# Rotary partners of the index heads fetched two tiles to a transfer, and a sixth scratch buffer

## The chip, the core and the metric

The kernel runs on one core of one Trainium2 chip. The metric is the device time of one execution in microseconds (us). The core's engines run side by side: PE (TensorE: matmuls, with PEld its weight loads), DVE (VectorE), ACT (ScalarE), POOL (GpSimd), and SP, which computes nothing here and only issues DMAs. Each engine and each issue queue works through its own list in order; semaphores tie the lists together. An instruction that waits holds up all that stands behind it on its engine.

## What is computed

Two transformer blocks run one after the other over 256 tokens of width 2048, in float32. The first has latent attention, a gated convolution and two output projections. The second, where the change lies, puts 16 meta tokens in front (T = 272 columns) and has a sparse attention, whose keys are chosen by a small indexer, and a gated recurrence. Cut to the indexer:

```python
h = rms_norm(x, norm_g); proj = h @ w_in
q_a, k_a, v_a, z_a, q_i, k_i, w_i, q_b, f_b, i_b, z_b, gates = jnp.split(proj, cuts, axis=-1)
qi = apply_partial_rope(q_i.reshape(B, T, 16, 64), *rope_i)      # 16 index heads of 64
ki = apply_partial_rope(rms_norm(k_i, idx_k_norm_g)[:, :, None, :], *rope_i)[:, :, 0, :]
score = jnp.einsum('bqhs,bqh->bqs', jax.nn.relu(jnp.einsum('bqhd,bsd->bqhs', qi, ki)), wi)
_, sel = lax.top_k(score, 64)                                    # then attention over sel
```

`apply_partial_rope` turns only the first 16 of a head's 64 elements: element j of the first 8 is combined with element j + 8, its partner, and the other way round. The other 48 pass through.

## The kernel before

Everything is held transposed, features on the 128 partitions and tokens along the row. A weight matrix comes in as units of up to 1024 columns by 128 partitions (512 KB): SP loads a unit into one of four `w_raw` buffers (`load`, L1259), ACT rounds it into `w_hi` (L1665), DVE forms the rest `w_lo` (L1973), and PE multiplies in three passes, hi by hi, hi by lo and lo by hi. A `load` waits for the `w_lo` of the unit four before it. A unit of this part is 24 matmuls of 256 or 272 columns.

The order of all engines' work is written by a planner, `plan_work`. `run` walks over the phases' units; when the last unit of a column group is done, `evac` puts the copies out of PSUM into the plan (for instance L2079 on DVE). After each unit `pump` is called once. It moves every active job one step on (a job is a Python generator, a step ends at a `yield`), then starts one job from the queue `pending`, if fewer than three are active. What a step adds is placed in the lists of all engines at that point. So a job's steps are one unit apart, and the queue is first come, first served.

The phases around the change are `qi` (one group of 8 tiles, 16 units), `ki` (2 units), `ka` (8), `va` (8), `qa2` (16), `fb` (16), `ib` (16). The 8 tiles of `qi` hold two index heads each; all are evacuated at the last `qi` unit. Then, for each tile, a job `rope_later("qi", k, ...)` is queued: a step that does nothing, then `rope_swap` (four DMAs on SP's queue, L1300, which copy the partner rows of the tile into a scratch buffer), an empty step, and `rope`. `rope` is one multiply by the sines on DVE (L2116, waits for the DMAs) and a multiply and an add on POOL (L2546, L2549). One tile's four DMAs are those of `SWAPS["qi"]`: for each half of 64 partitions one of 8 rows and one of 56 rows, 128 rows of 1024 bytes in all.

The job of the index key, `ki_job`, is queued at the `ki` evacuation. Its steps are: transpose, row sum, (empty), spread and normalise, (empty), `rope_key`. `rope_key` does the turn by two PE products (rotated, L1326 from `con`, and doubled), two DVE multiplies (L2124, L2126) and two DVE adds (L2130, L2131). At its end it queues the 16 jobs `index_head(h)`; each has a PE product that waits for the key (`done["ki", 0]`, the second add) and for its tile, an ACT relu, and, a step later, two DVE multiply-adds. The selection (DVE, 9 steps) follows the last index head, and queues the 8 attention heads `attention2`. Key heads (`ka_job`, 4) and query heads (`qa_job`, 8) are jobs too, queued at their evacuations. The recurrence is queued only after `qb`, a phase behind `ib`.

Scratch buffers come from `Ring(5)`: a step that needs one takes the next, and waits for the end of its last use. PSUM has five banks for products; a tile's first matmul waits until the tile that had the bank before is evacuated.

Of the kernel before, what the change touches and what calls it, by code (L numbers as in the profile page):

```python
# [9 lines left out]
F32R = mybir.dt.float32r  # L10
# [6 lines left out]
P = 128  # L17
D = 2048
KT = D // P
S = 256  # L20
NMETA = 16
T = S + NMETA
# [124 lines left out]
class Plan:  # L147
# [6 lines left out]
    def add(self, kind, *args, marks="", dma="", **of):  # L154
        s = Step(kind, args, of)
        for names, by in ((marks, 1), (dma, 16)):
            for name in names.split():
                self.count[name] = self.count.get(name, 0) + by
                s.raised.setdefault(name, []).append((self.sem(name), self.count[name]))
        self.steps.append(s)  # L160
        return s
# [105 lines left out]
def plan_work(sem):  # L267
    plan = Plan(sem)
    add, done = plan.add, plan.done
    ph = phases()  # L270
    units = plan.units = units_of(ph)
    banks, side, scratch, heads = Ring(5), Ring(3), Ring(5), Ring(3)
    stats, prob, prob_t, prob_m = Ring(6), Ring(2), Ring(2), Ring(2)
    issued, lows = {"load": 0, "split": 0}, deque()
    pending, active, deferred = deque(), [], deque()
# [132 lines left out]
    def rope_later(kind, k, ready, tables, rest=0):  # L408
        yield
        if kind == "kr":  # L410
            rope_key(kind, ready, tables)
        else:
            yield from rope(kind, k, ready, tables)
        for _ in range(rest):
            yield
# [18 lines left out]
    s = add("load_rows", dma="ld_pos " + "ld_rows " * 10 + "ld_meta", zero=zero)  # L434
    done["pos"], done["rows"], done["meta_in"] = s["ld_pos"], s["ld_rows"], s["ld_meta"]
    b = side.take()
    s = add("pre_cols", marks="pre_t pre_cols", bank=b, loaded=pre)
# [295 lines left out]
    s = add("meta_rest", marks="op_lo", head=done["meta_head"], high=done["meta_hi"])  # L733
# [49 lines left out]
    s = add("load_late", dma="ld_late ld_lvl")  # L783
# [20 lines left out]
    def evac_ki(g, m, pb, got):  # L804
        s = add("ki", marks="evac", pb=pb, got=got)
        pending.append(ki_job(s["evac"]))
        return s["evac"]

    def evac_qi(g, m, pb, got):
        k = m  # L810
        s = add("qi", k, marks="evac", pb=pb, got=got)
        pending.append(rope_later("qi", k, s["evac"], "late"))
        return s["evac"]

    def ka_job(k, t):
# [160 lines left out]

    pending.append(level_masks())
    run(ph["qi"], evac_qi)
    run(ph["ki"], evac_ki)
    run(ph["ka"], evac_ka)  # L980
# [79 lines left out]
ODD = 16  # L1060
H2_STEP, H2_AT, MG2_AT = 320, 32, 80
H2_LOW, H2_REST = 12, 33 * 64
# [8 lines left out]
class Memory:  # L1071


    def __init__(self, nc, ctx, a):
        def sb(name, shape, dt=F32):
            return ctx.enter_context(nc.sbuf_tensor(name, shape, dt))
# [5 lines left out]
        hb_all = sb("hb", [P, ODD + 2 * KT * S + ODD], F32R)  # L1082
        hb = hb_all[:, ODD:ODD + 2 * KT * S].rearrange("p (k n) -> p k n", k=2 * KT)
        self.hb_hi, self.hb_lo = hb[:, 0:KT, :], hb[:, KT:2 * KT, :]
        ob_all = sb("ob", [P, 2 * KT * (T + ODD)], F32R)
        ob = ob_all[:, H2_AT + NMETA:H2_AT + NMETA + 2 * KT * S].rearrange("p (k n) -> p k n", k=2 * KT)
        self.ob_hi, self.ob_lo = ob[:, 0:KT, :], ob[:, KT:2 * KT, :]
        mg2 = ob_all[:, MG2_AT:MG2_AT + 2 * KT * S].rearrange("p (k n) -> p k n", k=2 * KT)
# [8 lines left out]
        self.rope1 = sb("rope1", [P, 2, S])  # L1097
        self.fac = sb("factor", [P, 3, T])
        self.small = sb("small", [P, 256])
        self.scratch = [sb(f"scratch{i}", [P, T])[:, :] for i in range(5)]  # L1100
        self.heads = [sb(f"head_factor{i}", [P, T])[:, :] for i in range(3)]
        self.acc_a, self.acc_b = sb("acc_a", [P, S])[:, :], sb("acc_b", [P, S])[:, :]
        psum = [ctx.enter_context(nc.psum_tensor(f"bank{i}", [P, 512], F32))[:, :] for i in range(8)]
# [140 lines left out]
def sync_engine(nc, m, a, plan, S_):  # L1244

    sp, dma = Stream(nc.sync, None), nc.sync.dma_start
    rows = lambda ap: ap.rearrange("(k p) -> k p", p=P)

    def load_pre(s):
        sp.wait_ge(*s.of["zero"])  # L1250
        dma(m.rows_in[ROWS["pre"]:ROWS["pre"] + 16, :], rows(a["pre_norm_g"])).then_inc(S_("ld_pre"), 16)

    def load(s):
        i, = s.args
        u = plan.units[i]
        sp.wait_ge(*s.of["free"])
        src = m.weights[u.phase.weight].rearrange("(k p) n -> p k n", p=P)[:, u.k0:u.k0 + u.nk, u.c0:u.c0 + u.cols]
        dst = m.raw[:, i % N_RAW, 0:u.size].rearrange("p (k n) -> p k n", k=u.nk)
        dma(dst, src).then_inc(S_(f"raw{i % N_RAW}"), 16)  # L1259

    def load_con(s):
        dma(m.con[:, P:], a["const_f"][:, P:L0]).then_inc(S_("ld_con"), 16)

    def load_rows(s):
        dma(m.pos_i, a["positions"]).then_inc(S_("ld_pos"), 16)
        sp.wait_ge(*s.of["zero"])
        for name, src, n in (("post", rows(a["post_norm_g"]), 16), ("norm2", rows(a["norm_g_2"][0]), 16),
                             ("conv", a["conv_w"].rearrange("c (k p) -> (c k) p", p=P), 48),
                             ("qa", rows(a["q_a_norm_g"]), 4), ("kva", rows(a["kv_a_norm_g"]), 4),
                             ("lb", a["hgrn_lb_logits_2"].rearrange("l (k p) -> (l k) p", p=P), 16),  # L1270
                             ("qn", a["q_norm_g_2"], 1), ("kn", a["k_norm_g_2"], 1),
                             ("on", a["hgrn_out_norm_g_2"], 1), ("ikn", a["idx_k_norm_g_2"], 1)):
            dma(m.rows_in[ROWS[name]:ROWS[name] + n, 0:src.shape[1]], src).then_inc(S_("ld_rows"), 16)
        dma(m.x_meta[0:NMETA, :], a["meta_tokens_2"]).then_inc(S_("ld_meta"), 16)

    def load_x_again(s):
        sp.wait_ge(*plan.done["mg_z"])
        sp.wait_ge(*plan.done["x_kept"])
        dma(m.XR.rearrange("p k n -> p (k n)"), m.x_dram).then_inc(S_("ld_xagain"), 16)

    def x1_keep(s):
        sp.wait_ge(*plan.done["x1", KT - 1])
        dma(m.x1_dram, m.XR.rearrange("p k n -> p (k n)")).then_inc(S_("ld_x1kept"), 16)

    def load_late(s):
        sp.wait_ge(*plan.done["mg", KT - 1])
        dma(m.late, a["const_f"][:, L0:CONSTS["late"][1]]).then_inc(S_("ld_late"), 16)
        dma(m.lvl_in, a["const_lvl"]).then_inc(S_("ld_lvl"), 16)

    def load_x1_back(s):  # L1290
        sp.wait_ge(*plan.done["x1_kept"])
        sp.wait_ge(*plan.done["mg2_z"])
        dma(m.xT2.rearrange("p k n -> p (k n)"), m.x1_dram).then_inc(S_("ld_x1back"), 16)

    def rope_swap(s):
        x, use = m.rope_of(*s.args)[0], s.of["scratch"]
        sp.wait_ge(*use.after)
        sp.wait_ge(*s.of["ready"])
        for to, of, n in SWAPS[s.args[0]]:
            dma(m.scratch[use.slot][to:to + n, 0:x.shape[1]], x[of:of + n, :]).then_inc(S_(f"ld_rot{use.slot}"), 16)  # L1300

    def out2(s):
        g, blk = s.args
        sp.wait_ge(*s["evac"])
        w = slice(g * 512, (g + 1) * 512)
        dma(a["out"][0, blk * P:(blk + 1) * P, w], m.OT[:, blk, w]).then_inc(S_("ld_out"), 16)

    def end(s):
        sp.wait_ge(*s.of["stored"])

    does = dict(load_pre=load_pre, load=load, load_con=load_con, load_rows=load_rows, load_x_again=load_x_again,
                x1_keep=x1_keep, rope_swap=rope_swap, load_late=load_late, load_x1_back=load_x1_back, out2=out2, end=end)
    for s in plan.steps:
        if s.kind in does:
            does[s.kind](s)
# [1357 lines left out]
```

## Time and profile before

| | us |
|---|---|
| median of 3 runs | 1908.15 |
| lowest, highest | 1906.74, 1909.43 |
| the profiled execution's own time | 1908.92 |
| its span, first to last instruction | 1907.6 |
| PE busy | 1890.0 (99%) |
| DVE, ACT, POOL busy | 1174.7 (62%), 880.1 (46%), 323.6 (17%) |
| DMA | 347.31 MB, mean 182 GB/s |

A timeline row reads: start in us, length in us, engine, line of the kernel, operation, what it writes <- what it reads, count; in brackets, the time for which the engine was idle before it, and what ended that. `SPq` is SP's issue queue; its rows are the time that issuing takes, not the transfer. The rows of the DMA issue table show the weight loads as 512.0 KB each, landing 3.8 us after their issue.

### The profile page before, as it was taken

The numbers are of one execution on the slowest core, as the hardware profiler recorded it, in microseconds if no ns is written. First come the engines' busy times: TensorE is split into PE (matmuls) and PEld (weight loads), VectorE is DVE, ScalarE is ACT, GpSimd is POOL, SyncE is SP. The second block draws the span as 40 slices with busy tenths as digits, with TensorE's granted clock in tenths as the row PEclk, the third lists the DMA queues.
The fourth block names the chain that finished last, engine by engine and source line by source line (L and its number), as shares of the span: only waits on it lengthen the run. The fifth ranks groups of instructions, "written<-read, shape, count | busy, mean of one in ns | idle before, by whom it ended". The sixth has DMA issues, their size and how long they took to land.

```text
span 1907.6 us, 37116 instructions
## 1 busy us (share of the span) xinstructions
PE 1890.0 (99%) x15758; PEld 1857.5 (97%) x15758; DVE 1174.7 (62%) x1709; ACT 880.1 (46%) x1265; POOL 323.6 (17%) x317
## 2 busy tenths in 40 slices
PE   9999999999999999999999999999999999999999
PEld 8999999999999999999999999999999999999987
DVE  7765665656554556755654766676467776655744
ACT  6544454544444444544454543446443333444543
POOL 3220110202110003400221243040011132110300
PEclk9999999999999999999999999999999999999999
DMA  7566555566666666666565565563564444666664
GB/s 262 165 211 182 158 154 165 167 188 191 197 191 195 198 190 188 194 204 193 196 232 195 177 217 168 149 178 119 156 187 140 138 141 142 183 199 195 193 232 154
DMA packets 180752, 347.31 MB, mean 182 GB/s; under 512 B 11742, under 2 KB 24410, under 8 KB 180058
## 3 DMA queue, kind: packets, MB, share of 16 engines
q1 hardware_dynamic: 178938, 340.67, 58.8%
q10 hardware_dynamic: 1648, 4.26, 0.6%
q8 instruction: 124, 2.03, 0.4%
q14 instruction: 42, 0.34, 0.1%
HBM read 334.89 MB, written 6.29 MB: 179 GB/s over the span
## 4 chain that ended last, share of the span: by engine, by line
PE 92%; DVE 3%; SPq 1%; issue 1%; DMA 1%; ACT 1%; POOL 1%; POOLq 0%; ACTq 0%; DVEq 0%
PE bank L1326 91%; DVE w_lo L1973 1%; SPq L1300 1%; DMA scratch<-arena 1%; DMA w_raw<-in_w_in 1%; ACT w_hi L1665 1%; DVE hb L2215 0%; SPq L1259 0%; POOL stats L2533 0%; DVE arena L2079 0%; DVE scratch L2079 0%; ACT L1733 0%; POOL scratch L2583 0%; PE bank L1547 0%; ACT ob L1825 0%
## 5 line engine op out<-in xcount | busy, mean ns | idle before, releaser
L1973 DVE TENSOR_TENSOR w_lo<-w_raw,w_hi 128x1024 fp32r<-128x1024 f32 (+2 forms) x644 | 792.8, 1235 | 460.5 <-ACT w_hi L1665 458.6
L1665 ACT ACTIVATE w_hi<-w_raw 128x1024 fp32r<-128x1024 f32 (+2 forms) x644 | 662.8, 1032 | 854.5 <-PE bank L1326 839.7
L1326 PE MATMUL bank<-hb,w_hi 128*128 128x256 f32 x5284 | 954.5, 278 | 1.7 <-DVE hb L1997 1.6
L1326 PEld LDWEIGHTS bank<-hb,w_hi 128*128 128x128 f32 x5284 | 813.8, 188 | 3.7 <-DVE w_lo L1973 2.2
L1326 PE MATMUL bank<-ob,w_hi 128*128 128x256 f32 (+1 forms) x4060 | 767.7, 283 | 5.0 <-DVE ob L2269 1.7
L1326 PE MATMUL bank<-hb,w_lo 128*128 128x256 f32 x2448 | 677.5, 277 | 0.0
L1326 PEld LDWEIGHTS bank<-ob,w_hi 128*128 128x128 f32 x4060 | 633.2, 188 | 9.1 <-DVE w_lo L1973 2.3
L1326 PE MATMUL bank<-ob,w_lo 128*128 128x256 f32 (+1 forms) x2224 | 621.6, 279 | 0.0
L1326 PEld LDWEIGHTS bank<-hb,w_lo 128*128 128x128 f32 x2448 | 460.9, 188 | 0.0
L1326 PEld LDWEIGHTS bank<-ob,w_lo 128*128 128x128 f32 x2224 | 418.4, 188 | 0.0
L1326 PE MATMUL bank<-w_hi,ob 128*128 128x512 f32 (+1 forms) x384 | 104.4, 359 | 1.0 <-DVE arena L2079 1.0
L1326 PE MATMUL bank<-arena 128*128 128x64 f32 (+4 forms) x578 | 89.9, 296 | 1.0 <-POOL arena L2623 1.0
L2593 POOL TENSOR_TENSOR arena<-scratch,arena 128x256 f32<-128x256 f32 x32 | 38.4, 1229 | 258.7 <-DVE scratch L2079 258.7
L1326 PEld LDWEIGHTS bank<-w_hi,ob 128*128 128x128 f32 x384 | 66.9, 188 | 12.2 <-DVE arena L2079 1.4
L1326 PEld LDWEIGHTS bank<-arena 128*128 128x128 f32 x578 | 74.3, 191 | 3.0 <-issue 1.2
L2079 DVE TENSOR_TENSOR scratch<-bank,factor 128x256 f32<-128x256 f32 (+1 forms) x132 | 52.4, 421 | 30.7 <-PE bank L1326 30.6
L1326 PE MATMUL bank<-w_lo,ob 128*128 128x512 f32 (+1 forms) x192 | 68.4, 356 | 0.0
L2566 POOL TENSOR_TENSOR arena<-arena,factor 128x256 f32<-128x256 f32 x16 | 19.2, 1233 | 257.6 <-DVE arena L2079 257.6
L2583 POOL TENSOR_TENSOR scratch<-scratch,head_factor 128x256 f32<-128x256 f32 x16 | 12.5, 784 | 225.2 <-ACT head_factor L1783 225.2
L2079 DVE TENSOR_TENSOR arena<-bank,factor 128x256 f32<-128x256 f32 (+1 forms) x86 | 34.1, 418 | 18.2 <-PE bank L1326 18.2
L1326 PEld LDWEIGHTS bank<-w_lo,ob 128*128 128x128 f32 x192 | 36.1, 188 | 5.8
L2586 POOL TENSOR_TENSOR arena<-scratch,arena 128x256 f32<-128x256 f32 x32 | 39.6, 1237 | 2.5
(241 smaller groups left out, 1019.6 us busy)
## 6 DMA issues: line engine op xcount, KB each, us to landing
w_raw<-in_w_in SPq DMA_DIRECT2D x436, 512.0 KB, 3.8
w_raw<-in_w_out SPq DMA_DIRECT2D x64, 512.0 KB, 4.2
w_raw<-in_w_o_conv SPq DMA_DIRECT2D x32, 512.0 KB, 4.0
w_raw<-in_w_o_mla SPq DMA_DIRECT2D x32, 512.0 KB, 4.0
w_raw<-in_w_branch SPq DMA_DIRECT2D x32, 512.0 KB, 4.4
w_raw<-in_w_kv_b SPq DMA_DIRECT2D x16, 512.0 KB, 4.6
w_raw<-in_w_q_b SPq DMA_DIRECT2D x16, 384.0 KB, 3.5
arena<-x_kept SPq DMA_DIRECT2D x2, 2048.0 KB, 9.0
```

What stands on the lines that cost most here:

```text
L1300: dma(m.scratch[use.slot][to:to + n, 0:x.shape[1]], x[of:of + n, :]).then_inc(S_(f"ld_rot{use.slot}"), 16)
L1326: return nc.tensor.matmul(dst, lhsT, rhs, start=start, stop=stop, skip_group_check=True)
L1665: act(dst, src, ACT.Copy).then_inc(S_("w_hi"), 1)
L1973: tt(low, src, high.bitcast(F32), ALU.subtract).then_inc(S_("w_lo"), 1)
L2079: tt(dst, m.proj[s.of["pb"]][:, 0:dst.shape[1]], factor, ALU.mult).then_inc(S_("evac"), 1)
L2566: tt(m.u_t[:, t, :], m.u_t[:, t, :], m.R, ALU.mult).then_inc(S_("conv_b"), 1)
L2583: tt(z, z, ring[s.of["head"].slot][:, 0:S], ALU.mult).then_inc(S_("silu"), 1)
L2586: tt(y, z, y, ALU.mult).then_inc(S_("gated"), 1)
L2593: tt(y, m.scratch[s.of["scratch"].slot][:, 0:S], y, ALU.add).then_inc(S_("merged"), 1)
```

## The change

The scratch ring has six buffers instead of five, and all six lie in one tensor, so that two neighbours can be named in one access pattern. `ob` is cut from 9216 to 8992 columns, which it doesn't use. The eight `rope_later("qi", ...)` jobs are replaced by one job, `index_ropes`, queued after the last tile's evacuation. After an empty step it goes over the tiles in pairs: it takes two neighbouring scratch buffers (never the last with the first), adds `rope_pair`, an empty step, and then the two `rope` steps of the pair, followed at once by the next pair's `rope_pair`. `rope_pair` issues four DMAs for two tiles, each with twice the bytes in as many rows of partitions. DVE's and POOL's work on a tile is as it was.

```diff
-    banks, side, scratch, heads = Ring(5), Ring(3), Ring(5), Ring(3)
+    banks, side, scratch, heads = Ring(5), Ring(3), Ring(6), Ring(3)
...
+    index_tiles = []
+
+    def index_ropes():
+
+        yield
+        for k in range(0, 8, 2):
+            sc = scratch.take()
+            while sc.slot == 5:
+                sc.ends(sc.after)
+                sc = scratch.take()
+            sc2, landed = scratch.take(), f"ld_rot{sc.slot}"
+            t = add("rope_pair", k, dma=f"{landed} " * len(SWAPS["qi"]), scratch=sc, scratch2=sc2, ready=index_tiles[k + 1])
+            yield
+            yield
+            for j, use in ((k, sc), (k + 1, sc2)):
+                st = add("rope", "qi", j, marks="rope_sin rope_out", scratch=use, ready=index_tiles[j], landed=t[landed],
+                         tables="late")
+                use.ends(st["rope_out"])
+                done["qi", j] = st["rope_out"]
+
     def evac_qi(g, m, pb, got):
         k = m
         s = add("qi", k, marks="evac", pb=pb, got=got)
-        pending.append(rope_later("qi", k, s["evac"], "late"))
+        index_tiles.append(s["evac"])
+        if k == 7:
+            pending.append(index_ropes())
         return s["evac"]
...
-        ob_all = sb("ob", [P, 2 * KT * (T + ODD)], F32R)
+        ob_all = sb("ob", [P, H2_AT + (KT + H2_LOW) * H2_STEP], F32R)
...
-        self.scratch = [sb(f"scratch{i}", [P, T])[:, :] for i in range(5)]
+        self.scratches = sb("scratch", [P, 6 * T]).rearrange("p (k n) -> p k n", k=6)
+        self.scratch = [self.scratches[:, i, :] for i in range(6)]
...
+    def rope_pair(s):
+        k, = s.args
+        use, use2 = s.of["scratch"], s.of["scratch2"]
+        sp.wait_ge(*use.after)
+        sp.wait_ge(*use2.after)
+        sp.wait_ge(*s.of["ready"])
+        for to, of, n in SWAPS["qi"]:
+            dma(m.scratches[to:to + n, use.slot:use.slot + 2, 0:S], m.QI[of:of + n, k:k + 2, :]).then_inc(S_(f"ld_rot{use.slot}"), 16)
```

## Rows read from the trace of the kernel before

**Rows 1.** The page's head and its first section: busy time and share.

```profile
span 1907.6 us, 37116 instructions
PE 1890.0 (99%) x15758; PEld 1857.5 (97%) x15758; DVE 1174.7 (62%) x1709; ACT 880.1 (46%) x1265; POOL 323.6 (17%) x317
```

**Rows 2.** Waits of PE, whole span: who for whom, us, times, longest.

```profile
PE bank L1326 <- DVE arena L2079: 2.7, 4, 1.1
...
PE bank L1326 <- ACT rope L1885: 1.5, 1, 1.5
...
PE bank L1326 <- POOL stats L2533: 0.6, 3, 0.2
```

**Rows 3.** Timeline of PE, 1143 to 1158 us: its idle stretches (in brackets).

```profile
1149.05 0.52 PE L1326 MATMUL bank<-ob,w_hi 128*128 128x272 f32 x2 [1.08 <-DVE arena L2079]
...
1151.43 0.52 PE L1326 MATMUL bank<-ob,w_hi 128*128 128x272 f32 x2 [0.59 <-DVE arena L2079]
...
1156.40 0.81 PE L1326 MATMUL bank<-con,stats 128*128 128x128 f32 x6 [0.24 <-POOL stats L2533]
```

**Rows 4.** Timeline of SP's queue, 1119 to 1152 us: issues of partners (L1300) and weights.

```profile
1119.25 3.09 SPq L1300 DMA_DIRECT2D scratch<-arena  x4
...
1134.84 0.54 SPq L1259 DMA_DIRECT2D w_raw<-in_w_in  x1
1135.48 2.99 SPq L1300 DMA_DIRECT2D scratch<-arena  x4
...
1147.39 2.99 SPq L1300 DMA_DIRECT2D scratch<-arena  x4
```

**Rows 5.** Timeline of ACT, 1130 to 1136 us: one `w_hi` per unit.

```profile
1130.94 1.06 ACT L1665 ACTIVATE w_hi<-w_raw 128x1024 fp32r<-128x1024 f32 x1 [1.98 <-PE bank L1326]
1133.98 1.06 ACT L1665 ACTIVATE w_hi<-w_raw 128x1024 fp32r<-128x1024 f32 x1 [1.98 <-PE bank L1326]
```

**Rows 6.** Timeline of DVE, 1146 to 1152 us.

```profile
1148.12 0.43 DVE L2116 TENSOR_TENSOR scratch<-scratch,arena 128x256 f32<-128x256 f32 x1 [1.61 <-DMA scratch<-arena]
...
1148.56 0.78 DVE L2079 TENSOR_TENSOR arena<-bank,factor 128x272 f32<-128x272 f32 x2
...
1151.76 0.43 DVE L2116 TENSOR_TENSOR scratch<-scratch,arena 128x256 f32<-128x256 f32 x1
```

**Rows 7.** Chain of work, in order of time: single issues of one tile (start, us).

```profile
1128.10 0.67 SPq L1300
1128.82 0.79 SPq L1300
```

**Rows 8.** Timeline of SP's queue elsewhere: partners of 32-row and of 16- and 112-row pieces.

```profile
84.61 2.42 SPq L1300 DMA_DIRECT2D scratch<-arena  x4
...
1163.93 1.18 SPq L1300 DMA_DIRECT2D scratch<-arena  x2
```

**Rows 9.** Timeline, 1164 to 1168 us, PE and DVE: the index key's `rope_key`.

```profile
1164.65 0.72 PE L1326 MATMUL bank<-arena 64*128 64x272 f32 x2
...
1165.41 0.44 DVE L2124 TENSOR_TENSOR scratch<-bank,arena 128x272 f32<-128x272 f32 x1 [1.98 <-PE bank L1326]
...
1165.76 0.38 PE L1326 MATMUL bank<-con,stats 128*128 128x128 f32 x1
...
1166.86 0.44 DVE L2131 TENSOR_TENSOR arena<-arena,scratch 64x272 f32<-64x272 f32 x1
```

**Rows 10.** Timeline of POOL, 1125 to 1132 us: two adds of `rope`.

```profile
1125.91 0.73 POOL L2549 TENSOR_TENSOR arena<-arena,scratch 128x256 f32<-128x256 f32 x1
...
1129.88 1.60 POOL L2549 TENSOR_TENSOR arena<-arena,scratch 128x256 f32<-128x256 f32 x1
```

**Rows 11.** Timeline of ACT, 1290 to 1300 us: two table loads and attention's copy.

```profile
1290.61 1.28 ACT L1895 ACT_TABLE_LOAD   x1
...
1296.02 1.28 ACT L1733 ACT_TABLE_LOAD   x1
...
1299.55 0.36 ACT L1885 ACTIVATE rope<-bank 16x256 f32<-16x256 f32 x1
```

More of the change, by code:

```diff
@@ L1311, in sync_engine @@
     does = dict(load_pre=load_pre, load=load, load_con=load_con, load_rows=load_rows, load_x_again=load_x_again,
-                x1_keep=x1_keep, rope_swap=rope_swap, load_late=load_late, load_x1_back=load_x1_back, out2=out2, end=end)
+                x1_keep=x1_keep, rope_swap=rope_swap, rope_pair=rope_pair, load_late=load_late, load_x1_back=load_x1_back, out2=out2, end=end)
     for s in plan.steps:
```

## The prediction

> **What bounds the kernel now.** I read the page's head first. PE is busy 1890.0 of 1907.6 us [rows 1]; an engine at 99% sets the end, and nothing shortens the kernel unless PE idles less or has less to do. The change takes no matmul away and adds none. So the whole question is PE's idle time, and the second view is the list of PE's waits: it is short, and three of its lines can be touched by this change: 2.7 us behind DVE's evacuations, 1.5 us behind an ACT copy, 0.6 us behind POOL's small powers [rows 2]. The third view is PE's timeline around the index heads. There PE idles 1.08 us and 0.59 us at the start of phase `va`, each ended by an evacuation on DVE, and 0.24 us a little later, ended by POOL [rows 3]. Together 1.91 us. This is what the change can win where it stands.
>
> **Why PE idles there.** A unit of `ka` takes 3.04 us: ACT's `w_hi` of one unit follows that of the unit before by 1133.98 - 1130.94 [rows 5]. In each unit SP must issue one weight load, 0.54 us, and one tile's partners, 2.99 us, with 0.1 us between rows: about 3.65 us in a 3.04 us unit [rows 4]. So SP falls behind. The eight groups of partners begin at 1119.25 and end their series at 1147.39, 28.1 us for 7 steps, against 7 x 3.04 = 21.3 us of units: SP is 6.9 us late at the last [rows 4]. DVE's multiply of a tile comes two units after its issue is due, 6.1 us, so late partners reach DVE when it already waits: 1.61 us for the seventh tile, until 1148.12 [rows 6]. Behind that multiply in DVE's list stand the evacuations of `ka`, which run at 1148.56 and free the banks that `va` wants; PE resumes at 1149.05 [rows 3, 6]. The chain is: SP's issues, the DMA, DVE in order, the bank, PE.
>
> **SP's half.** The change halves the number of these issues, from 32 to 16. What one of the new ones costs the trace of before doesn't show. Nearest rows: an issue for 8 rows takes 0.67 us, one for 56 rows 0.79 us, seven times the bytes and the rows for 0.12 us more [rows 7]; four issues of 32 rows take 2.42 us, two of 16 and 112 rows 1.18 us [rows 8]. Bytes and rows hardly count, the number of issues does. So I take 3.0 us for a pair, as for one tile before; the other end is twice that, 6.0 us, if the second segment in each row doubles it; below 3.0 only a little can be had (2.4, as the 32-row pieces). With 3.0 us, SP has per two units two loads and one pair, 2 x 0.64 + 3.0 = 4.3 us, in 6.1 us: it no longer falls behind.
>
> The Trainium skill speaks against this ("DMA: Bandwidth & Descriptors", section "Issuing engines are not separate DMA queues"): the sequencer's time to start a DMA is usually small beside the DMA itself. By that rule the partners would be late for their transfer, pairing them would win nothing, and the 1.91 us would stay. The rows here disagree: 2.99 us of issuing per tile in a unit of 3.04 us, and the last tile's multiply starts 1.4 us after the last issue ends [rows 4, 6].
>
> **The new order of the pumps.** Call the pump after the last `qi` unit pump 0; `ki` is evacuated before pump 2, `ka` before pump 10, `va` before 18, `fb` before 42 and 50. Counting steps gives, before: partners of tile k at pump k + 1, its `rope` at k + 3, up to 10; key's transpose at 9 (its job had to queue behind the tiles), `rope_key` at 14, the first index head at 17, since two key heads' jobs were ahead. After: pairs at pumps 1, 3, 5, 7, ropes at 3, 5, 7, 9, from one slot of three. The key's job starts at once: transpose at 3, row sum 4, spread 6, `rope_key` at 8. And in that same pump the first index head starts, because nothing else is queued. The 16 heads run at pumps 8 to 23, one each; the key heads' jobs, which queue behind them, start at 24 instead of 10, and the first attention head at 48 instead of 49. The recurrence is queued only after `qb`, so nothing behind moves, and no drain gets longer.
>
> **What goes.** The last pair's partners are issued at pump 7 and used at 9, before `ka` is evacuated, with SP on time. DVE has no reason to hold back the evacuations: -1.08 - 0.59 us. The key's powers are asked for at pump 4 and used at 6, no longer behind the eighth tile's POOL work: -0.24 us [rows 3]. Sum -1.9 us. What is late next is nothing on PE's list in that stretch but the following.
>
> **What comes.** The first index head's product now stands directly behind the two products of `rope_key` on PE, and waits for the key that DVE makes of them. In the trace `rope_key` starts at 1164.65, PE is free for its next matmul at 1165.76, and DVE's second add ends at 1166.86 + 0.44 = 1167.30 [rows 9]. Before, other units' matmuls stood in between (three pumps). Now PE waits 1167.30 - 1165.76 = 1.54, with some 0.06 us for the semaphore 1.6 us. All matmuls of the unit behind stand behind this wait. That is the lower bound, with DVE free and POOL quiet. POOL is still at the ropes of tiles 4 and 5 at about that time; its adds take 0.73 us alone and 1.60 us beside DVE [rows 10], so an add of DVE's may be held for one such POOL instruction, about 0.9 us: upper bound 2.5 us. I take 1.8 us, near the lower end, since DVE idled 1.98 us ahead of the key before [rows 9] and POOL should be nearly through.
>
> The Trainium skill has the sharing as a lock ("SBUF — State Buffer", section "SBUF: two separate sides"): a DVE instruction with two SBUF operands and a POOL instruction that reads SBUF exclude each other for a whole instruction. Only L2130 and L2131 have two SBUF operands, so by that rule the stall is either 1.6 us or one POOL instruction longer, not in between. The lengthening of POOL's add agrees with it in kind [rows 10].
>
> **Attention.** PE's 1.5 us behind ACT's copy L1885 [rows 2] is the first attention head's mix, which waits for the copy that ends at 1299.91 [rows 11]. ACT was late there because `fb`'s second group was evacuated (sigmoids, L1895) between the exponentials of the first two heads, so that the tables were switched twice in 7 us, 1.28 us each [rows 11]. After the change the heads start one pump earlier: both exponentials come before the sigmoids, and the first head's copy has only one switch and four sigmoids ahead of it. I take the 1.5 us as won; the bounds are -1.5 and 0, with a new place for the same stall between.
>
> **The rest** is priced at nothing. DVE's and POOL's work on tiles is the same, only in twos: two multiplies of 0.43 us [rows 6] in every second unit, under 3.04 us of matmuls. The index heads' two multiply-adds move from `va` and `qa2` to `ka` and `va`, one head per unit as before. DVE is busy 62% [rows 1], and that is the cover; where it fails, an evacuation is late and PE pays what DVE is late, as in rows 3. A sixth scratch buffer removes waits on scratch buffers, of which PE's list has none [rows 2]. The weights' and operands' buffers `w_*`, `hb` and `ob` begin where they did; `arena` and what follows moves, which could cost or gain something that no row bounds; I give it the tails.
>
> **The sum.** -1.9 + 1.8 - 1.5 = -1.6 us, on the profiled execution's own 1908.92 us (span 1907.6 and 1.3 around it): 1907.3. The median of the runs is 0.8 us lower than that execution, 1908.15, so by medians 1906.6 us.
>
> **The rivals.** (A) *Attention's stall stays or moves by a unit.* Its cause would be ACT's load in general, and the order of one head would not matter. For it: the first heads of attention still meet `fb`'s evacuation within two units. Sum -0.1 us: 1908.1. (B) *A pair costs SP twice as long,* 6.0 us: the slower side. The point from which it decides is where two loads and a pair exceed two units, 6.1 - 1.3 = 4.8 us for a pair. Then pairs start at about 1119.3, 1126.4, 1133.6 and 1140.8. The third ends its issue at 1139.6, lands 1.4 us later at 1141.0, and DVE's multiplies of tiles 4 and 5 end at 1141.9. The key's step is at pump 8, two units after 1133.98 [rows 5], at 1140.1, its first product 0.76 us later [rows 9], at 1140.8: PE's new wait grows by 1.1 us to 2.9. The fourth lands at 1148, as late as before, so the 1.67 us stay. Sum +2.9 - 0.2 - 1.5 = +1.2 us: 1909.3. Against it: rows 7 and 8. (C) *The key's wait is hit by POOL* at the upper bound, 2.5 us, with A: -1.9 + 2.5 = +0.6: 1908.7. (D) *Partners don't matter* (the skill's rule above; or the evacuations are late for another reason): the 1.9 us stay and the new wait comes, +1.8 - 1.5 = +0.3 us: 1908.4.
>
> **How the numbers follow.** The measurement tells 0.2%, 3.8 us, from no change; all these sums are inside it. Forecast 0.5, A 0.17, B 0.08, C 0.08, D 0.07; the remaining 0.1 is for what no row bounds (moved buffers, another stall by the new order), half of it each way and most of that beyond 3.8 us. That gives faster 0.06, same 0.88, slower 0.06. Range: the lowest sum is -1.9 + 1.6 - 1.5 = -1.8, the highest case +1.2; the three runs of before lie down to 1.4 us below and up to 1.3 us above their median by the table of times, and half a us below is for what is priced at nothing: 1908.15 - 1.8 - 1.4 - 0.5 = 1904.4, and 1908.15 + 1.2 + 1.3 = 1910.6. The tail beyond, and the cases it cuts, are under 2 in 10.
>
> **What would show each step.** Right: SP's issues of a pair take about 3.0 us and start at pump times, 6.1 us apart; no wait of DVE L2116 over 1 us after the first pair; no idle of PE behind L2079 at `va`'s start. PE idles 1.6 to 2.5 us once, ended by DVE L2131, eight units after `qi`'s last product. PE's row behind ACT L1885 is gone. Wrong: pairs of 4.8 us or more (B); the same bank waits with SP on time (D); a wait behind L1885 of over 1 us (A); or a change of PE's mean time per matmul, which would be the moved buffers and not the order.

## The result, and the profile after

The changed kernel takes 1917.1 us (median of 4 runs, 1914.5 to 1920.0) against 1908.2 us: a ratio of 1.0051, 95% interval 1.0039 to 1.0063. It is slower, and outside the range of the prediction. Its profiled execution took 1915.34 us (span 1914.0), 6.4 us more than that of before. The profiled execution lies 1.8 us below the median of its four runs; the account below is of the profiled 6.4 us, and what the other three lost on top isn't profiled. Five more runs of it later gave a median of 1916.1 us.

The page's head of the kernel after, beside [rows 1]:

```profile
span 1914.0 us, 37092 instructions
...
PE 1895.1 (99%) x15758; PEld 1862.0 (97%) x15758; DVE 1176.8 (61%) x1709; ACT 879.6 (46%) x1265; POOL 320.6 (17%) x317
```

The number of matmuls is the same, 15758, and yet PE is busy 5.1 us longer. Of the 6.4 us only 1.3 are additional idle time. That is the first thing to see: a reading that asks only who waits for whom can't find most of the loss.

PE's waits after (who for whom, us in total, times, longest), beside [rows 2]:

```profile
PE bank L1358 <- ACT rope L1917: 1.8, 1, 1.8
PE bank L1358 <- DVE arena L2163: 1.7, 1, 1.7
...
PE bank L1358 <- ACT head_factor L1888: 0.9, 1, 0.9
...
PE bank L1358 <- DVE arena L2111: 0.7, 1, 0.7
PE bank L1358 <- DVE scratch L2111: 0.6, 2, 0.4
```

L2079 of before is L2111 here, L1885 is L1917, L2131 is L2163: the file is 32 lines longer. The bank waits on DVE fell from 2.7 to 0.7 us, and none is left at the start of `va`. The wait for the index key is new. Attention's wait behind L1917 is still there, and three waits stand in phase `fb` and at the start of `ib` that were not there before (L1888 once, L2111 on `scratch` twice).

SP's queue after, beside [rows 4] (start, length, instruction, count):

```profile
1120.63 3.38 SPq L1332 DMA_DIRECT2D scratch<-arena  x4
...
1138.98 3.23 SPq L1332 DMA_DIRECT2D scratch<-arena  x4
```

The four pairs cost SP 3.2 to 3.6 us each, where one tile cost 3.0 to 3.1. SP has issued the last partners at 1142.2 instead of 1150.4.

Timeline of PE, DVE and POOL after at `rope_key`, beside [rows 9]:

```profile
1143.48 0.44 DVE L2156 TENSOR_TENSOR scratch<-bank,arena 128x272 f32<-128x272 f32 x1 [1.31 <-PE bank L1358]
...
1144.02 0.72 POOL L2578 TENSOR_TENSOR arena<-arena 128x256 f32<-128x256 f32 x1 [1.25 <-DMA scratch<-arena]
1144.49 0.55 DVE L2162 TENSOR_TENSOR arena<-arena,scratch 64x272 f32<-64x272 f32 x1
1145.05 0.44 DVE L2163 TENSOR_TENSOR arena<-arena,scratch 64x272 f32<-64x272 f32 x1
...
1145.64 0.94 PE L1358 MATMUL bank<-arena 128*128 128x144 f32 x4 [1.73 <-DVE arena L2163]
```

The first index head's product waits 1.73 us. The first of DVE's two adds lies beside a POOL instruction and took 0.55 us, the second 0.44. The Trainium skill ("SBUF — State Buffer", section "SBUF: two separate sides") would have DVE wait for the end of that POOL instruction at 1144.74, some 0.25 us; the rows show 0.11, though a POOL row's end is rough.

Timeline of ACT and PE after at the first attention heads, beside [rows 11]:

```profile
1293.78 1.28 ACT L1927 ACT_TABLE_LOAD   x1
1295.07 0.75 ACT L1927 ACTIVATE arena<-scratch 128x272 f32<-128x272 f32 x2
1297.10 0.43 ACT L1927 ACTIVATE arena<-scratch 128x272 f32<-128x272 f32 x1 [1.28 <-DVE scratch L2111]
...
1299.44 0.36 ACT L1917 ACTIVATE rope<-bank 16x256 f32<-16x256 f32 x1
...
1299.94 0.67 PE L1358 MATMUL bank<-probT,arena 128*128 128x256 f32 x2 [1.79 <-ACT rope L1917]
```

Both exponentials now come before the sigmoids, as forecast. But the sigmoids wait for DVE's evacuation of `fb`'s last tiles (1.28 us), and the first head's copy stands behind them in ACT's list all the same.

**Where PE is busy longer.** The windows view counts PE's matmuls in a stretch (start:end, length, PE busy and number, granted clock, DMA share, GB/s). Three stretches, in `qb`, in `zb` and in `gb`, none with a change of phase but for the first 0.85 us of the second in the kernel after, which still belong to `ba`. The kernel before:

```profile
1370.00:1400.00 30.00, 30.00 (x268) 1.00 0.66 196
1640.00:1660.00 20.00, 20.00 (x179) 1.00 0.63 183
1700.00:1760.00 60.00, 60.00 (x532) 1.00 0.66 192
```

The kernel after:

```profile
1370.00:1400.00 30.00, 30.00 (x257) 1.00 0.59 175
1640.00:1660.00 20.00, 20.00 (x172) 1.00 0.65 188
1700.00:1760.00 60.00, 60.00 (x532) 1.00 0.66 195
```

PE is never idle in any of them, and the granted clock is 1.00, the 2.4 GHz level, in all. Still PE does 11 matmuls fewer in 30 us of `qb`, and 7 fewer in 20 us of `zb`. Start to start, a matmul of 256 columns takes 113.3 ns in the one case and 117.8 ns in the other. Apart from a few matmuls at a change, every stretch of such matmuls at the full clock has one of these two paces; PE can keep one for many units. I call them pace 113 and pace 118. In the second block nearly every change lies at a small product among the tiles or at a pause. Neither is needed, though. In the first block, from 113 to 155 us, PE works without a pause through blocks of 12 matmuls, each with the two operands in the other order than the one before, and its pace turns at every second border of blocks, in every profile. The last such turn in the kernel after, from 12 matmuls in 1.36 us to 12 in 1.41:

```profile
153.40 0.39 PE L1358 MATMUL bank<-w_hi,ob 128*128 128x256 f32 x2
...
154.76 0.40 PE L1358 MATMUL bank<-hb,w_hi 128*128 128x256 f32 x2
...
156.17 0.40 PE L1358 MATMUL bank<-hb,w_hi 128*128 128x256 f32 x2
```

And in `before_again`, `order_single` and `apart_gap_skip` the pace fell from 113 to 118 between two units of `qi`, near 1080.8 us, with neither a small product nor a pause there.

A unit of 24 matmuls costs 0.11 us more at 118. Matmuls of 272 columns (`ki`, `ka`, `va`, `fb`, `ib`) have one pace, 126.5 ns.

The time from PE's first matmul of one stretch of phases to that of the next gives a budget. Profiled executions, us against before:

| | `fb`, `ib` | `qb` | `ga` to `ba` | `zb` to `bb` | `ki` to `qa2` | all ahead of `ki` |
|---|---|---|---|---|---|---|
| length in before | 123.13 | 44.94 | 229.43 | 175.49 | 122.68 | 1114.13 |
| after | +2.1 | +1.6 | +0.7 | +1.2 | -0.2 | +1.0 |
| before, again | 0.0 | 0.0 | -0.2 | +4.8 | +0.2 | +0.5 |
| after, again | +2.1 | +1.6 | +0.6 | +1.2 | +1.7 | 0.0 |
| layout_only | 0.0 | 0.0 | +0.4 | +0.8 | -0.9 | -0.3 |
| layout_ring6 | 0.0 | +1.6 | +0.7 | +0.8 | +0.2 | -1.4 |
| key_apart | 0.0 | +1.6 | +0.6 | +0.8 | -2.7 | -0.5 |
| apart_gap_skip | +0.4 | 0.0 | -0.1 | 0.0 | -2.7 | +0.7 |

The change touches nothing ahead of `ki` but the addresses, and the last column scatters from -1.4 to +1.0 without order; I read nothing from it.

### The profile page after: what moved, and what is told of

Read it like the earlier page. It is cut to its first block, busy times and chain, and to the rows that moved or that the text cites. A ratio compares the mean times of both kernels' runs of the same rounds, so it can differ in the third digit from the quotient of the medians.

```text
span 1914.0 us, 37092 instructions
## 1 busy us (share of the span) xinstructions
PE 1895.1 (99%) x15758; PEld 1862.0 (97%) x15758; DVE 1176.8 (61%) x1709; ACT 879.6 (46%) x1265; POOL 320.6 (17%) x317
## 4 chain that ended last, share of the span: by engine, by line
PE 92%; DVE 4%; DMA 1%; ACT 1%; issue 1%; SPq 0%; POOL 0%; DVEq 0%; POOLq 0%; ACTq 0%
PE bank L1358 91%; DVE w_lo L2005 2%; DMA w_raw<-in_w_in 1%; DVE arena L2294 1%; DMA scratch<-arena 0%; ACT w_hi L1697 0%; SPq L1323 0%; DVE ob L2301 0%; DVE arena L2111 0%; DVE arena L2288 0%; ACT ob L1857 0%; DVE scratch L2148 0%; POOL scratch L2615 0%; PE bank L1579 0%; DVE scratch L2111 0%
## 5 line engine op out<-in xcount | busy, mean ns | idle before, releaser
L2625 POOL TENSOR_TENSOR arena<-scratch,arena 128x256 f32<-128x256 f32 x32 | 38.4, 1231 | 258.7 <-DVE scratch L2111 258.7
L2111 DVE TENSOR_TENSOR scratch<-bank,factor 128x256 f32<-128x256 f32 (+1 forms) x132 | 52.5, 422 | 31.8 <-PE bank L1358 31.8
L2111 DVE TENSOR_TENSOR arena<-bank,factor 128x256 f32<-128x256 f32 (+1 forms) x86 | 34.0, 419 | 19.1 <-PE bank L1358 19.1
L2565 POOL TENSOR_TENSOR stats<-stats,con 128x2 f32<-128x2 f32 (+2 forms) x18 | 19.1, 1060 | 152.9 <-DVE stats L2040 152.9
```

What stands on the lines that cost most here:

```text
L2111: tt(dst, m.proj[s.of["pb"]][:, 0:dst.shape[1]], factor, ALU.mult).then_inc(S_("evac"), 1)
L2565: tt(f if keep is None else keep, f, m.c("neg_half")[0:w, :].to_broadcast([w, len(starts)]), ALU.pow).then_inc(S_("rf_pow"), 1)
L2625: tt(y, m.scratch[s.of["scratch"].slot][:, 0:S], y, ALU.add).then_inc(S_("merged"), 1)
```

## The experiments

All ratios are against runs of the kernel before on the same chip, with 95% intervals. `before_again` and `after_again` are the two kernels unchanged.

> The kernel before, unchanged, profiled again. Its profile showed two paces of PE for matmuls of 256 columns: 113 ns from start to start in most phases, 118 ns in others (most of qi, parts of ga, za). Theory 1 (the pace is drawn anew in each execution): which phases are slow differs from the first profile. Theory 2 (the pace follows from the kernel's own order and addresses): the same phases are slow again, qi at 118 ns, qb and zb at 113 ns. Time 1.000 of the kernel before in both.

Measured: median 1909.99 us (1906.1 to 1915.1), 1.0010 (1.0000 to 1.0021) of itself. So this comparison can be off by 0.1%, and by its interval up to 0.2%. In its profiled execution, 1914.18 us, the windows view shows this, the last line for `gb`:

```profile
1150.00:1155.00 5.00, 5.00 (x31) 0.67 0.70 236
...
1700.00:1760.00 60.00, 60.00 (x512) 1.00 0.64 187
```

512 matmuls in 60 us of `gb` instead of 532: pace 118 from a pause at the start of `gb` to the end of `bb`, 4.8 us in one stroke, with not one instruction changed. From `qb` on to there the paces are those of the first profile in all but two units. It would account for the executions of before that take 1913 us, of which none is profiled beside this one. The line above it shows a second thing that varies: after 1.0 us of idle time at `va`'s start the granted clock was 0.67 over these 5 us, part of them at the 1.2 GHz level.

> The changed kernel, unchanged, profiled again. In its first profile qb and zb ran at 118 ns per matmul instead of 113, about 2.3 and 3.2 us of the 6.4 us by which it was longer, and PE idled 1.7 us for the index key. Theory 1 (pace drawn in each execution): another set of slow phases, and the times of single runs spread over some 5 us. Theory 2 (pace set by order and addresses): qb and zb slow again. Time 1.003 to 1.006 of the kernel before in both; PE's wait for the key, 1.7 us, is there in both.

Measured: median 1916.14 us (1913.8 to 1916.8), 1.0035 (1.0022 to 1.0047). With the four first runs the loss is 0.35 to 0.5%. Its pace pattern is that of the first profile, phase by phase. But `ki` to `qa2` took 1.9 us more; its windows there:

```profile
1140.00:1145.00 5.00, 2.95 (x19) 1.00 0.72 227
1145.00:1150.00 5.00, 5.00 (x27) 0.66 0.36 107
```

PE waited 2.05 us for the key, and behind that wait the granted clock was 0.66: 27 matmuls in 5 us, where the 126.5 ns pace gives 39. 12 matmuls fewer are 1.5 us. With the wait of 2.05 us the key then costs 3.5 us.

> The kernel before with only the addresses changed: ob cut, scratch buffers in one tensor of six of which the ring uses five. With the ring of six too, the time was 1.0023 of before and qb, part of ba and most of zb ran at 118 ns per matmul. Theory A (what matters is which scratch buffer the last transposes before qb read): qb at 113 ns again, time 1.000 to 1.001, with zb slow if zb's pace hangs on the moved statistics. Theory B (the moved addresses set the pace): qb and zb at 118 ns, 1.002 to 1.003.

```diff
-        ob_all = sb("ob", [P, 2 * KT * (T + ODD)], F32R)
+        ob_all = sb("ob", [P, H2_AT + (KT + H2_LOW) * H2_STEP], F32R)
...
-        self.scratch = [sb(f"scratch{i}", [P, T])[:, :] for i in range(5)]
+        self.scratches = sb("scratch", [P, 6 * T]).rearrange("p (k n) -> p k n", k=6)
+        self.scratch = [self.scratches[:, i, :] for i in range(6)]
```

> The kernel before with the buffers alone changed: ob cut, six scratch buffers in one tensor, a ring of six; jobs and DMAs as before. If the moved buffers or the sixth buffer are the cause, this takes the 6 to 9 us, with qb and zb at 118 ns: 1.003 to 1.005. If the order of the steps is the cause, it is 1.000 (within 2 us), with phases paced as in the kernel before.

The same edit on before, and `Ring(5)` made `Ring(6)`. Measured: `layout_only` 1909.25 us, 1.0010 (1.0001 to 1.0019); `layout_ring6` 1911.92 us, 1.0023 (1.0013 to 1.0032). The windows of `qb` and `zb`, first `layout_only`:

```profile
1370.00:1400.00 30.00, 30.00 (x267) 1.00 0.66 193
1640.00:1660.00 20.00, 20.00 (x172) 1.00 0.58 169
```

then `layout_ring6`:

```profile
1370.00:1400.00 30.00, 30.00 (x257) 1.00 0.63 183
1640.00:1660.00 20.00, 20.00 (x172) 1.00 0.63 186
```

The moved addresses alone put the end of `ba` and most of `zb` at pace 118; the sixth buffer puts `qb` there too. Neither kernel has another order of work, another job or another DMA. So a loss of 0.23% comes without the pairs. By the comparison of before with itself the 0.10% of `layout_only` can't be told from nothing; what its budget shows, +0.4 and +0.8 us, can, since every kernel at these addresses shows it.

> The changed kernel with three empty steps between the index key's turn and the queueing of the 16 index heads, so that the first head no longer stands directly behind the key on PE. The 1.7 us idle of PE behind DVE's add should be gone. If that wait is the main cause, most of the 6 to 9 us goes: 1.001. If the pace of PE is the main cause, only some 2 us go in themselves, and the rest depends on which phases are slow in this order: anything from 0.999 to 1.005, to be told by the phases' pace.

```diff
 (at the end of the index key's job, between rope_key and the index heads)
+        yield
+        yield
+        yield
```

Measured: 1910.13 us (1908.7 to 1913.2), 1.0007 (0.9998 to 1.0015), against 1.0035 to 1.0051 of after. Of PE's waits in this kernel one is of attention:

```profile
PE bank L1361 <- ACT rope L1920: 1.5, 1, 1.5
```

The key's wait is gone, and with three steps more the attention heads are back in their old place: the waits in `fb` and `ib` are those of before, 1.5 us and no more. From 1112 to 1240 us PE waits for nobody. `ki` to `qa2` is 2.7 us shorter than before and 2.5 shorter than after, `fb` and `ib` 2.1 shorter than after. So the pairs do what they should; the order that came with them gave it all back and more. What is left, `qb` +1.6, `ga` to `ba` +0.6, `zb` to `bb` +0.8, is pace.

> The changed kernel with its order of steps and its buffers, but each pair's partners fetched by eight one-tile DMAs in place of four two-tile ones. If the pairing of the DMAs is worth what the forecast said, SP falls behind as before, DVE waits for partners, and PE's wait for the index key grows from 1.7 to 3 us or more: 1 to 3 us longer than the changed kernel, 1.004 to 1.006. If the DMAs don't matter, it is as the changed kernel, 1.0035 to 1.005.

```diff
-        for to, of, n in SWAPS["qi"]:
-            dma(m.scratches[to:to + n, use.slot:use.slot + 2, 0:S], m.QI[of:of + n, k:k + 2, :])...
+        for j, u in ((0, use), (1, use2)):
+            for to, of, n in SWAPS["qi"]:
+                dma(m.scratch[u.slot][to:to + n, 0:S], m.QI[of:of + n, k + j, :])...
```

Measured: 1917.79 us, 1.0054 (1.0042 to 1.0067). Its SP queue and its PE waits from 1112 to 1240 us:

```profile
1128.29 6.00 SPq L1334 DMA_DIRECT2D scratch<-arena  x8
```

```profile
PE bank L1360 <- DVE arena L2165: 3.3, 1, 3.3
```

Eight issues take 6.0 us, four with twice the bytes 3.2: a pair saves SP 2.8 us. In the old form but the new order the partners are late, and the key waits 3.3 us instead of 1.7 to 2.05. This is what my rival B described (a pair of 6.0 us, a wait of 2.9 us), except that the bank waits at `va` did not stay; that DVE catches up in the 3.3 us is my reading, not shown. The Trainium skill's rule that a DMA's issuing is small beside the transfer ("DMA: Bandwidth & Descriptors", section "Issuing engines are not separate DMA queues") doesn't hold for these DMAs: with the bytes and the order unchanged, the number of issues moved PE's wait by 1.3 to 1.6 us. In total time `order_single` can't be told from after (1.0035 to 1.0051).

> The kernel before, addresses and ring of five unchanged, but one scratch buffer is skipped ahead of ib's second group, so that the last transposes before qb read buffers 3, 4, 0, 1 in place of 2, 3, 4, 0. No instruction is added. Theory A (which buffer they read sets qb's pace): qb at 118 ns, 15 units of 24 matmuls by 4.4 ns = 1.6 us longer, 1.001. Theory B (addresses as a whole): qb stays at 113 ns, 1.000.

```diff
             if name == "ib" and k == 4:
+                skip = scratch.take()
+                skip.ends(skip.after)
```

On before, with its ring of five: one buffer is passed over, so that all later users get another one. Measured: 1907.55 us, 0.9999 (0.9990 to 1.0008); every stretch from `fb` on within 0.15 us of before. Another buffer as such does nothing in a ring of five.

> The changed kernel with three scratch buffers skipped ahead of ib's second group, so that the last transposes before qb read buffers 2 to 5 instead of 5, 0, 1, 2. With the ring of six qb ran at 118 ns, with the ring of five at 113 ns, whichever buffers were read. Theory A (with a ring of six, the buffers read there set qb's pace): qb turns to 113 ns, 1.6 us shorter than the changed kernel. Theory B (something else that the ring of six shifts, the moment at which PE goes on): qb stays at 118 ns, or turns by chance of the shift.

The same edit on after, with three buffers passed over. Measured: 1913.04 us, 1.0028 (1.0018 to 1.0037). Windows of `qb` and `zb`:

```profile
1370.00:1400.00 30.00, 30.00 (x267) 1.00 0.61 180
1640.00:1660.00 20.00, 20.00 (x172) 1.00 0.63 187
```

`qb` is back at pace 113, +0.0 us against before instead of +1.6, and `zb` is not. I took this as proof that the buffers' numbers decide `qb`; the last experiment took that back.

> The changed kernel with the key and the first index head three steps apart (as in key_apart, 1.0007), and an unused gap of 64 bytes behind the scratch buffers, so that all behind them (head factors, sums, probabilities, the last statistics) lies 256 bytes, not 192, further than in the kernel before. Theory A (ba and zb are slow for the moved head factors and statistics, which the last small products before them read): the end of ba and zb turn to 113 ns, 2 us shorter, 0.9997. Theory B (another cause): ba and zb at 118 ns as in key_apart, 1.0007.

```diff
+        sb("gap", [P, 16])
```

On `key_apart`: 64 bytes are left free behind the scratch tensor, so all that follows lies 64 bytes further. Measured: 1912.02 us, 1.0014 (1.0003 to 1.0025), with the fastest run at 1907.0. Windows of `qb`, `zb` and `gb`:

```profile
1370.00:1400.00 30.00, 30.00 (x257) 1.00 0.62 187
1640.00:1660.00 20.00, 20.00 (x179) 1.00 0.61 184
1700.00:1760.00 60.00, 60.00 (x512) 1.00 0.62 189
```

`zb` and the end of `ba` are back at pace 113, as in before, and `qb` is not. `gb` and `bb` had the pace 118 that the unchanged kernel also showed once, 4.8 us, and so this profile is no faster. Its 12 runs fall into two groups, 4 from 1907.0 to 1908.9 us and 8 from 1911.1 to 1914.5; the profiled one, 1912.4, is of the slower.

> The changed kernel with one small extra product (two float32 matmul passes, about 0.5 us) behind the second unit of qb and of zb, where no other small product runs. Theory (PE falls into one of two paces at a small product and keeps it until the next): in both phases the pace can change exactly there, and only there; if it turns to 113 ns, qb gets 1.5 us shorter and zb 1.5 us, net 1 to 2 us shorter than the changed kernel; if it falls back to 118 ns, 1 us longer. Rival (the phases are slow for their own reads of buffers or weights): the pace is 118 ns before and behind the product.

```diff
+            if p.name in ("qb", "zb") and i - p.first == 1:
+                warm(1)
+                for _ in range(2):
+                    skip = side.take()
+                    skip.ends(skip.after)
```

> The kernel before with the same small extra product behind the second unit of qb and of zb that took qb in the changed kernel from 118 to 113 ns. In the kernel before both phases run at 113 ns. Theory (a small product or a pause can set either pace): it costs its 0.5 us twice, and the pace behind it either stays 113 ns (+1 us) or falls to 118 ns in one of them (+1.5 us more). If the pace were a property of the phase's own reads, it would stay at 113 ns. The place of any change is exactly the product.

One small product more, whose result nobody reads, after the second unit of `qb` and of `zb`; two side banks are passed over so that later users keep theirs. On after (`kick`): 1914.79 us, 1.0038 (1.0026 to 1.0051). On before (`kick_before`): 1910.91 us, 1.0020 (1.0008 to 1.0032). PE's timeline at the extra product, `kick`:

```profile
1369.93 0.40 PE L1363 MATMUL bank<-ob,w_hi 128*128 128x256 f32 x2
...
1370.99 0.40 PE L1363 MATMUL bank<-ob,w_hi 128*128 128x256 f32 x2
...
1372.05 0.59 PE L1363 MATMUL bank<-con 128*128 128x256 f32 x2
...
1373.52 0.39 PE L1363 MATMUL bank<-ob,w_hi 128*128 128x256 f32 x2
...
1374.54 0.39 PE L1363 MATMUL bank<-ob,w_hi 128*128 128x256 f32 x2
```

and `kick_before`:

```profile
1364.20 0.39 PE L1331 MATMUL bank<-ob,w_hi 128*128 128x256 f32 x2
...
1365.22 0.39 PE L1331 MATMUL bank<-ob,w_hi 128*128 128x256 f32 x2
...
1366.24 0.59 PE L1331 MATMUL bank<-con 128*128 128x256 f32 x2
...
1367.38 0.40 PE L1331 MATMUL bank<-ob,w_hi 128*128 128x256 f32 x2
...
1368.44 0.40 PE L1331 MATMUL bank<-ob,w_hi 128*128 128x256 f32 x2
```

Between the two rows of each pair lie nine matmuls. In `kick` they take 1.06 us (118 ns each) ahead of the extra product and 1.02 us (113 ns) behind it; in `kick_before` 1.02 us ahead and 1.06 behind. In `qb` the same product turned the pace one way in one kernel and the other way in the other, at its own place. So the pace is a state of PE that an interruption of the row of tiles can set. It need not: the second extra product of `kick`, in `zb`, left the pace at 118, and only a pause nine units later turned it to 113. In `kick_before` the one in `zb` turned 118 to 113. There the pace at the end of `ba`, ahead of that product, was 118 as well, at the addresses of before (`ga` to `ba` +1.1 us): the only edit ahead of that point is the product in `qb`, over 200 us earlier. `qb` cost +0.6 us instead of +1.6 in `kick`, and +1.9 instead of 0 in `kick_before`.

> The kernel after with all three countermeasures: three empty steps between rope_key and the index heads, a gap of 64 bytes behind the scratch tensor, and three scratch buffers passed over ahead of ib's second group. If what the change lost is what the earlier runs name, each loss has its own undoing: PE's key wait of 1.7 us and fb's waits go as in key_apart (ki to qa2 -2.7 us against before, fb and ib 0), ba's end and zb run at 113.3 ns per matmul as in pad_after, and qb does too as in skip6. Then the sum is about -2.5 to -4 us against before: ratio 0.998 to 0.9987. Rival: the pace of qb in skip6 came from that kernel's own order of the attention heads (one step earlier than here) and not from the buffers; then qb stays at 117.8 ns (+1.6 us) as in pad_after, and the ratio is 0.9990 to 1.0005.

> As apart_gap_skip, without the gap of 64 bytes. If the gap's addresses set the pace of ba's end and zb, these go back to 117.8 ns (eight or nine units of ba and eleven or more of zb, some +2 us against apart_gap_skip), as in key_apart: ratio 0.9990 to 1.0000 if qb is at 113.3 ns. Rival: ba's and zb's pace is set by what ran before them and not by addresses; then it may follow qb's and be 113.3 ns here too, and the two kernels are the same.

`key_apart` with `skip6`'s edit, and the first of them with `pad_after`'s gap as well. Measured: `apart_gap_skip` 1907.23 us (1905.6 to 1913.3), 1.0005 (0.9996 to 1.0014); `apart_skip` 1913.89 us (1910.4 to 1916.8), 1.0031 (1.0020 to 1.0042). Windows of `qb`, `zb` and `gb`, `apart_gap_skip`:

```profile
1370.00:1400.00 30.00, 30.00 (x267) 1.00 0.66 193
1640.00:1660.00 20.00, 20.00 (x179) 1.00 0.65 185
1700.00:1760.00 60.00, 60.00 (x532) 1.00 0.66 195
```

and `apart_skip`:

```profile
1370.00:1400.00 30.00, 30.00 (x257) 1.00 0.63 190
1640.00:1660.00 20.00, 20.00 (x172) 1.00 0.60 179
1700.00:1760.00 60.00, 60.00 (x512) 1.00 0.64 188
```

With all three edits every part of the loss is undone but a wait of 0.4 us in `ib`, and the profiled execution takes 1907.38 us, 1.5 less than before's. For `zb` the theory holds at the moved addresses: in each of the eight profiles (of seven kernels) without the gap its first eleven units or more lie at pace 118 (`kick`, where the extra product stands in it, not counted), in both with the gap it lies at 113. But `kick_before` has some of its units at 118 with no address moved, so the addresses aren't the only thing that decides. For `qb` it falls: the same three skipped buffers left it at 118 in `apart_skip` and not in `skip6` or `apart_gap_skip`. Buffers and addresses are not two separate causes. In time, `apart_gap_skip` is level with before and 0.3 to 0.5% faster than after. The ratio expected, 0.998 to 0.9987, holds neither for the median nor for the profiled execution (0.9992 of before's; from `ki` on it is 2.3 us shorter, and 0.7 longer ahead of it). It doesn't beat before. 7 of its 11 runs lie between 1905.6 and 1907.4 us, the other 4 between 1910.9 and 1913.3. The gap between the two groups is about the price of a slow `gb` and `bb`, 4.8 us, and `apart_gap_skip`'s profile, of the lower group, has them at pace 113, while `pad_after`'s, of its upper group, has them at 118. With one profile of each kernel, that this is the reason is argued, not shown.

## Why the prediction was wrong, point by point

**SP's half: right.** A pair costs 3.2 to 3.6 us and not 6.0, the pairs start 5.0, 6.3 and 7.0 us apart, SP is on time, the two bank waits of 1.67 us and POOL's 0.24 are gone in every kernel of the new order. `key_apart` shows the gain alone: -2.7 us against before's profile. The 0.8 us beyond my 1.9 are in no wait of the list. Against other profiles of before's order the same stretch gains between 1.1 (`kick_before`, -1.6) and 2.9 (`before_again`, +0.2), since the bank wait varies from one execution to the next; so the median of `key_apart` shows less of it.

**The key's wait: the size right, its consequence missed.** Forecast 1.8, measured 1.73 to 2.05 us. But in `after_again`, `kick` and `order_single` the granted clock fell to 0.66 or 0.74 over 5 us at the end of it, some 1.5 us more, and in the first profile and `skip6` it didn't. The order of before had such a fall too, in 3 of its 6 profiles, behind the bank wait at `va`. There it cost little: with PE slower behind the first wait, DVE caught up and the second, 0.59 us, didn't come (`before_again`: `ki` to `qa2` +0.2). I had counted 1.9 us of waits removed and 1.8 added as if a us of idle time had one price. That DVE catches up is argued from the missing second wait.

**Attention's 1.5 us: wrong.** This is rival A, to which I gave 0.17. The step that failed is "the first head's copy has only one switch and four sigmoids ahead of it". I took the length of the work in front and not the time at which it could run: the sigmoids wait for DVE's evacuation, so the copy started at 1299.44 us where it had started at 1299.55, and PE waited 1.79 us. The one step earlier also put a query head's squares on ACT behind `fb`'s first evacuation (0.88 us, L1888) and an evacuation late for its bank (0.26 and 0.38). Instead of -1.5 the term was +1.8 by the waits and +2.1 by the budget. "Nothing behind moves" and "the rest is priced at nothing" did not hold here, where 16 jobs and all that queues behind them shift.

**Moved buffers: the tails, and the largest part of the loss.** This is the other step that failed: a term put at nothing. I gave it 0.1 in all, together with any other stall, although the prediction itself named PE's mean time per matmul as the sign that would show them. By the budget `qb`, `ga` to `ba` and `zb` to `bb` cost +3.4 us. Layout and ring alone, with before's order, cost +3.1 us there (`layout_ring6`), and 0.23% in time (medians 1911.9 and 1908.4 us). The rest isn't the buffers': pace 118 in nine units of `qa2` instead of one, 8 x 0.11 = 0.9 us, stands in all five profiles of the new order without the empty steps, and not in `layout_only`, `layout_ring6` or `key_apart`. That part of the pace came with the order of the steps.

**The sum redone** from the same profile: -1.9 (waits at `va`) + 1.7 (key) + 2.1 (`fb`, `ib`) + 0.9 (pace in `qa2`) - 0.9 (rest of `ki` to `qa2`, not traced) + 3.5 (from `qb` on, pace) + 1.0 (ahead of `ki`, by chance as far as seen) = 6.4 us, against 6.42 measured. Forecast was -1.6; of the error of 8.0 us attention is 3.6, the pace from `qb` on 3.5, the pace in `qa2` 0.9. The range failed because each end was made of sums over waits, and none of them had a term for PE's own rate.

**What stays open.** Why one small product leaves PE at 113.3 ns and the next at 117.8 ns. Order, buffers and a gap of 64 bytes each change it at some places, and in the first block a swap of operands does; the intervals between PE's matmuls ahead of `qb` differ by a few ns between kernels of either pace. The Trainium skill says of the ports to SBUF that PE never waits on another engine there ("SBUF — State Buffer", section "SBUF: two separate sides"). By that, no other engine's traffic would be the cause of pace 118. `layout_only` shows pace 118 in `ba` and `zb` where before has 113, with addresses alone changed, but no run here shows whether a port is its cause. The pairs with a ring of five at the old addresses, which might have kept `qb` and `zb` as they were, weren't tried.

## What to carry to other kernels

When PE is busy 99% of the time, count its matmuls in equal stretches with no idle time in both kernels before explaining a few us by waits: a change of rate by 4% shows there and in no list of waits. A job queue that is first come, first served passes every shift on; after shortening one job, put empty steps where later jobs need their old places (three lines undid the key's wait, `fb`'s waits and the slow units of `qa2` here). And a change below 0.5% that moves buffers wants a control with the moved buffers alone, and several profiles of each kernel.

## What the runs showed of the hardware

- Matmuls of 256 columns run start to start at 113.3 or 117.8 ns at the same granted clock of 1.00. Pace 118 lasted up to 45 units without a break (4.8 us in `gb` and `bb` of `before_again`). The same small product turned it in either direction in two kernels (`kick`, `kick_before`), and it also turned where blocks of 12 matmuls swap their operands (113 to 155 us), and in three profiles between two units with nothing in between.
- Idle time of 1.0 to 3.3 us on PE around 1145 us was followed by a granted clock of 0.66 to 0.79 in a stretch of 5 us in some executions and not in others of the same kernel (`after` and `after_again`, `before` and `before_again`). In the four kernels without that idle time it never came.
- Four SBUF-to-SBUF DMA issues of 128 rows took 3.0 us, four with two segments of 1 KB in each row 3.2 us, eight 6.0 us: the cost goes by the number of issues, some 0.75 to 0.8 us each.
